# Four levels of a chunked recurrence: products over packed query columns

## What is computed

```python
b = jnp.cumsum(gc, axis=2)                       # log decays, summed inside a chunk
o = jnp.einsum('bhtk,bhkv->bhtv', qc * jnp.exp(b), s)
decay = jnp.exp(jnp.where(tri, b[:, :, :, None, :] - b[:, :, None, :, :], -jnp.inf))
att = jnp.einsum('bhtk,bhtsk,bhsk->bhts', qc, decay, kc)
o = o + jnp.einsum('bhts,bhsv->bhtv', att, vc)
s = jnp.exp(b_end)[..., None] * s + jnp.einsum('bhsk,bhsv->bhkv', kc * jnp.exp(b_end[:, :, None, :] - b), vc)
```

## Time and profile before

| | |
|---|---|
| median of 3 runs | 2225.09 us (2222.95 to 2227.34) |
| the profiled execution | 2226.52 us |
| its span | 2224.7 us |
| PE busy in the span | 2108.2 us (95%) |
| PEld, DVE, ACT, POOL busy | 85%, 51%, 36%, 40% |
| mean granted clock of PE | 0.974 |
| the recurrence (first product to last chunk of head 3) | 986.0 to 1096.9 us |

### The profile page before, as it was taken

The page is one execution under the profiler, slowest core; times in us unless marked ns, Lnnn a source line. Parts: engine busy times, 40 slices in busy tenths (PEclk is TensorE's granted clock), DMA queues, the critical chain, the costliest instruction groups (busy, mean ns, idle before and its releaser), DMA issues. The chain is left out here.

```text
span 2224.7 us, 38518 instructions
## 1 busy us (share of the span) xinstructions
PE 2108.2 (95%) x15606; PEld 1881.6 (85%) x15606; DVE 1145.7 (51%) x2132; ACT 793.7 (36%) x1654; POOL 880.8 (40%) x631
## 2 busy tenths in 40 slices
PE   5998999999999999998899999999999999999998
PEld 3997888856777689987899999678999999997886
DVE  5116545355676710258530054666865665654558
ACT  3203222234655611336412221234333333333553
POOL 2322121011111131211211223364388788776785
PEclk9999999988999999998899999999999999999999
DMA  7564534283100051100322130321244434357762
GB/s 267 193 214 160 183 121 152 92 304 139 32 32 11 1 143 39 39 9 3 99 76 57 47 125 4 117 95 41 86 162 151 139 132 166 129 182 284 266 226 105
DMA packets 152760, 268.23 MB, mean 121 GB/s; under 512 B 17817, under 2 KB 86348, under 8 KB 147975
## 3 DMA queue, kind: packets, MB, share of 16 engines
q1 hardware_dynamic: 144375, 222.70, 30.0%
q0 software_dynamic: 8208, 43.07, 5.5%
HBM read 211.93 MB, written 58.08 MB: 121 GB/s over the span
## 5 line engine op out<-in xcount | busy, mean ns | idle before, releaser
L3518 PE MATMUL PS<-down_parts 128*128 128x512 f32 x924 | 211.7, 390 | 1.1 <-DVE down_parts L4091 1.1
L3518 PEld LDWEIGHTS PS<-down_parts 128*128 128x128 f32 x924 | 173.1, 188 | 38.7 <-issue 2.0
L3475 PE MATMUL PS<-part_hi,w_ring 128*128 128x258 f32 x1152 | 192.3, 285 | 0.0
L3475 PEld LDWEIGHTS PS<-part_hi,w_ring 128*128 128x128 f32 x1152 | 162.1, 191 | 4.3 <-issue 4.3
L3475 PE MATMUL PS<-sum_blocks,w_ring 128*128 128x258 f32 x1296 | 161.6, 285 | 1.9 <-DVE out_sums L4041 1.9
L3475 PEld LDWEIGHTS PS<-sum_blocks,w_ring 128*128 128x128 f32 x1296 | 159.7, 192 | 2.1 <-DVE out_sums L4041 2.1
L651 POOL TENSOR_TENSOR w_merge_parts<-w_merge_raw,w_merge_parts 128x1024 fp32r<-128x1024 f32 x24 | 59.3, 2496 | 202.4 <-ACT w_merge_parts L644 183.6
L3867 POOL TENSOR_TENSOR down_parts<-down_raw,down_parts 128x512 fp32r<-128x512 f32 x71 | 118.5, 1686 | 43.2 <-ACT down_parts L3673 42.9
L2399 PE MATMUL PS<-h_hi,w_merge_parts 128*128 128x344 f32 x768 | 131.9, 324 | 0.0
L2399 PEld LDWEIGHTS PS<-h_hi,w_merge_parts 128*128 128x128 f32 x768 | 122.5, 189 | 3.1 <-issue 3.0
L1865 ACT ACTIVATE scores<-scores,mins_p 128x640 f32<-128x640 f32 (+5 forms) x192 | 112.5, 589 | 25.2 <-DVE mins_p L1907 24.4
(11 more groups left out here) (617 smaller groups left out, 5182.9 us busy)
## 6 DMA issues: line engine op xcount, KB each, us to landing
down_raw<-act_blocks SPq DMA_DIRECT2D x77, 256.0 KB, 3.4
w_or_ada<-w_ada SPq DMA_DIRECT2D x8, 2048.0 KB
w_raw<-w_up SPq DMA_DIRECT2D x11, 1024.0 KB, 9.4
w_raw<-w_gate SPq DMA_DIRECT2D x11, 1024.0 KB, 6.7
w_down_rows<-w_down SPq DMA_DIRECT2D x11, 1024.0 KB, 7.3
w_down_blocks<-w_down_sums SPq DMA_DIRECT2D x11, 1024.0 KB, 8.7
down_raw<-w_down_blocks SPq DMA_DIRECT2D x44, 256.0 KB, 4.0
act_blocks<-act_sums SPq DMA_DIRECT2D x10, 1024.0 KB, 5.1
```

What stands on the lines that cost most here:

```text
L3475: last = pe.matmul(out[:, c, :], r32(w[:, k, :]), r32(h[:, k, QUART * c:QUART * c + QUART]), start=first and k + i == 0, stop=k == 3 and i ...
L3518: last = pe.matmul(PS[:, t, c], r32(s[:, x, P * (t % 4):P * (t % 4) + P]), r32(s[:, y, c]), start=first and i == 0, stop=last_j and i == 2 ...
```

## The change

Levels 3 to 6 multiply each chunk's 128 columns of `X` by the query columns alone: the 64 columns that stand in the second halves of the blocks, read with strides (`pair_halves(...)[1]`). They are written side by side, 64 for each chunk, so a job's 8 outputs lie in one PSUM bank. Each of these levels' masks keeps only its query columns too (64 wide, behind the two masks of 128), and `pick` reads mask and PSUM packed, and writes into `att` with strides as before. Levels 0 to 2, 7 and 8, and the order of all work, stay.

```diff
-    lev = [lev[0] | lev[1] | lev[2]] + lev[3:] + [s == t]
-    c["c_levels"] = np.stack(lev, 1).astype(np.int32)
+    small = [x.reshape(P, -1, 2, h)[:, :, 1].reshape(P, P // 2) for x, h in zip(lev[3:], (8, 4, 2, 1))]
+    c["c_levels"] = np.concatenate([lev[0] | lev[1] | lev[2], s == t] + small, 1).astype(np.int32)
...
-        lev = at("levels", [P, LEV - 1, P], 139104, I32)
+        lev = at("levels", [P, 4 * P], 139104, I32)
...
+        HALFC = P // 2
...
-            sp.dma_start(lev[:, :, :], a["c_levels"][:, :, :]).then_inc(lev_in, 16)
+            sp.dma_start(lev[:, :], a["c_levels"][:, :]).then_inc(lev_in, 16)
...
                             out = PS[:, 2 * (U % 2) + c // 4, P * (c % 4):P * (c % 4) + P]
+                            if 3 <= w < 7:
+                                out = PS[:, 2 * (U % 2), HALFC * c:HALFC * c + HALFC].rearrange("p (n s) -> p n s", s=64 >> w)
...
                             elif w == 6:
-                                last = pe.matmul(out, kk[:, h, cc], X[:, n % 3, cc], start=True, stop=True)
+                                last = pe.matmul(out, kk[:, h, cc], pair_halves(X[:, n % 3, cc], w)[1], start=True, stop=True)
                             else:
-                                last = pe.matmul(out, X[:, n % 3, cc], X[:, n % 3, cc], start=True, stop=True)
+                                last = pe.matmul(out, X[:, n % 3, cc], pair_halves(X[:, n % 3, cc], w)[1], start=True, stop=True)
...
-                d, level = att[:, h % 2, :, :], lev[:, u, :].unsqueeze(1).to_broadcast([P, NT, P])
+                d = att[:, h % 2, :, :]
+                x = P if w == 7 else 0
+                level = lev[:, x:x + P].unsqueeze(1).to_broadcast([P, NT, P])
                 if w == 2:
                     d, level, src = (t[:, :, 16:] for t in (d, level, src))
                 elif w < 7:
-                    d, level, src = (t.rearrange("p c (n x s) -> p c n x s", x=2, s=64 >> w)[:, :, :, 1] for t in (d, level, src))
+                    d = d.rearrange("p c (n x s) -> p c n x s", x=2, s=64 >> w)[:, :, :, 1]
+                    level = lev[:, 2 * P + HALFC * (w - 3):2 * P + HALFC * (w - 2)].rearrange("p (n s) -> p n s", s=64 >> w).unsqueeze(1).to_broadcast([P, NT, HALFC // (64 >> w), 64 >> w])
+                    src = PS[:, 2 * (U % 2), :].rearrange("p (c n s) -> p c n s", c=NT, s=64 >> w)
```

## The result

The changed kernel takes 2252.73 us (median of 5 runs, 2246.38 to 2255.53) against 2225.09 us before: a ratio of 1.0123, with a 95% interval of 1.0102 to 1.0143. It is slower by 1.2%. The profiled execution took 2255.46 us, with a mean granted clock of 0.957 (0.974 before).

A forecast was written before the change was run, and what follows sets the result against it. Bound: two chains ending close together, PE to level 5 then ACT, and PE to level 7 then DVE. Terms -0.35 + 4.2 + 8.0 = +11.9 us gave 2238.4 us profiled, median 2237 us, range 2222 to 2248.

The forecast's parts named there:

- the number of lost heads: Later heads (1 to 3) staying at half clock from level 3 to level 7: 0 to 3, one taken as likeliest.
- -0.35: Levels 3 to 6 at full clock: weight loads set the pace, 0.07 us less per job, five jobs on the path.
- 4.2: Head 0: clock falls around levels 3 to 5, later levels run at half; 3.4 us for two levels, 5.1 for three.
- 8.0: Microseconds added by one later head that stays at half clock from level 3 to the end of level 7.
- two or three later heads: Rival: two or three of heads 1 to 3 stay at half clock; 2245 us or 2253 us, chance 0.20.
- a head that enters level 3 at half clock: Condition for a later head to stay slow: levels 3 to 6 have half the columns to climb back on.
- A head at full clock: Later heads entering the changed levels at full clock: 128-column chunks follow without a gap, so the clock was expected to hold.
- 22.4 us: Later head at half clock, level 3 to the end of level 7: this time in place of 14.0 us.
- the rows at 414 and 1147 us: Profile evidence elsewhere in the kernel: 64 columns and one column cost 107 ns alike, so weight loads set the pace.
- the rival by which the columns set the pace: Levels 3 to 6 take half of 1.78 us and the clock holds; 5.2 us faster, 2219.8 us, chance 0.07.
- The picks, masks and bank: Levels 3 to 6: shorter picks only lengthen DVE's waits, smaller masks and one PSUM bank change no wait; zero.
- The rule on idle gaps: Skill page blames gaps between matmul bursts; no new gap in PE, so unchanged clock; the prediction trusted the 414 us row instead.

The follow-up runs named there:

- the moved wait: The kernel before, with the wait for the stored state moved from a head's first state update to its second; 2225.41 us, 0.9999.
- with fillers: Changed kernel plus three unused 256-column products before levels 0, 1 of heads 1 to 3 and levels 3, 4 of head 0; 2228.51 us, 1.0024.
- with the clock held: Unused products before levels 0, 1 (heads 1 to 3) and 3, 4 (all heads), added to the changed kernel, 2222.01 us, and the kernel before, 2220.96 us.
- the first set of fillers: The kernel before plus three unused 256-column products ahead of levels 0 and 1 of heads 1 to 3; 2224.49 us, 0.9997.
- all of them: The kernel before plus unused 256-column products before levels 0, 1 of heads 1 to 3 and levels 3, 4 of all heads; 2220.96 us, 0.9974.

## Why the prediction was wrong

It said 2237 us, 2222 to 2248. The time is 2252.73, outside the range by 5 us: the direction and the mechanism were right, the number of lost heads was not.

- *The step that failed* is "So the number of such heads is 0 to 3, and I take one as the likeliest". It was three in the profiled execution. With three the same sum gives -0.35 + 4.2 + 3 x 8.0 = 27.85, 2254.4 us for the profiled execution, which took 2255.46. The rival "two or three later heads" with its 2253 us for three was thus the one that came true; I gave two or three heads a chance of 0.20 and left the case of three out of the range. That it meets the median to within 0.3 us is luck: the five runs lie between 2246.38 and 2255.53, the terms' errors cancel (head 0 cost 0.9 us more, the part behind head 3 took 0.7 us less), and only one run was profiled.
- *Why one was too few.* The prediction had the right condition, "a head that enters level 3 at half clock, as heads 2 and 3 do now", and the experiments bear it out. By this condition and its own rows two heads were to be lost, heads 2 and 3, and taking one was a discount without a row behind it. The third is head 1. Before, its clock fell at 1004.5, 3.2 us after the transposes of head 0, and was back before level 3, 10.9 us after them. After the change it fell at 1013.2, 4.3 us after the transposes, and level 3 began 11.3 us after them at half clock (1020.14, 3.65 us). In heads 2 and 3 the falls came 5.0 and 5.5 us after the transposes (1047.3 - 1042.33, 1081.5 - 1076.03), about as before (5.1 and 6.1), so nothing in a lost head helps the next one. That the delay of head 0 is what cost head 1 its early return is not shown, and one profile speaks against it: with heads 1 to 3 changed and head 0 not, the fall came earlier still, at 1000.50, and level 3 was entered at half clock all the same. With 128 columns throughout, head 1 entered level 3 at full clock in the profile before and at half in that of the moved wait (3.75 us), so its early return before was not a property of the kernel. What fixes when the clock falls and returns between levels 0 and 2 stays open.
- *A head at full clock.* "Each changed level is followed by a chunk of 128-column products and no gap, and I expect that to hold" is right for levels 5 and 6 (1.00 throughout) and held in head 2 of the kernel with heads 2 and 3 changed. It fails for levels 3 and 4, which have gaps at full clock (0.54 and 0.95 us in head 1 before), as the prediction itself says where they "wait for `X` from DVE": with fillers, head 1 fell there from full clock, while head 2 of the other kernel did not.
- *The price of a later head* was right: 8.0 taken; 8.1, 7.3 and 8.7 measured, 24.1 for three. From level 3 to the chunk behind level 7 I had 22.4 us; in head 1 it took 21.5 (1020.14 to 1041.66), as the clock came back inside level 7. *Head 0* was 4.2 taken, 5.1 measured (20.3 - 15.2): levels 5, 6 and 7 all ran at half clock, and most of level 4 too. That is the upper of the two values I had worked out (5.1).
- *The load pace.* Of the -0.35 nothing was seen: a job of 64 columns takes 1.73 to 1.82 us at full clock, one of 128 takes 1.78, and with the clock held the recurrence is 0.2 us shorter. The columns don't set it, as the rows at 414 and 1147 us said, and the rival by which the columns set the pace is out. At half clock I took 3.5 us; the start to start of two 64-column levels with a chunk between is 4.69 us in the trace after (1029.66 to 1034.35), which less 1.23 for the chunk is 3.46. Read to the start of its chunk, a level takes 3.31 us (1029.66 to 1032.97) and the chunk 1.38.
- *The picks, masks and bank* cost nothing, as said (masks only: 0.9999). The picks of levels 5 and 6 did not fall to 0.69 us, and with masks alone packed they take the same; what is left with strides is the write into `att`.
- *The rule on idle gaps.* The trace after has PE and PEld busy for 13.60 of 13.60 us at half clock. The Trainium skill, page TensorE: Matmul & The Clock Gate, section HAM oscillation — how this bites in real kernels, looks for the cause of a low clock in waits between bursts of matmuls, its example a wait for a DMA of about 3 to 5 us. The trace does not agree with that as the whole account: this stretch had no gap and stayed low, and in head 0 the clock held with waits of 1.37 and 1.44 us ahead of levels 3 and 4 of 128 columns and fell with 1.39 and 1.48 us ahead of those of 64. The prediction was right to let the row at 414 us weigh more. That the falls begin around waits is so here too, but they are shorter ones: 1.07 us before level 3 ahead of the fall in the kernel with fillers, 1.48 us before level 4 in head 0 after.

## What to carry to other kernels

Where weights change with every product, halving the moving columns leaves the time at full clock as it was and can cost the clock itself: look at the granted clock by stretches, and find the job in which it comes back after a gap, before making that job narrower. When a job is narrowed after the return and PE does not wait around it, nothing happened here; at full clock but with waits around it, the clock fell in head 0 each time and in one later head, while four others held. In the job of the return, each narrowed level runs on at half clock and all later waits shift with it. And if one unit of a repeated pattern can be lost, price the case in which all of them are, and keep it in the range.

## What was not expected of the hardware

- PE at half clock while never idle: 13.60 us of both matmul and weight load in 13.60 us (after), 25.9 and 25.1 of 27.2 us in head 1. Full weight loading neither kept the clock nor brought it back; in the later heads a level of 128 columns did, with the same loads.
- 128 columns and 64 columns with 128 x 128 float32 weights cost the same at full clock, 1.78 and 1.79 us for a job of 16.
- The predicated copy of 512 elements a partition took 0.68 to 0.72 us at levels 3 and 4 and 1.29 to 1.32 us at levels 5 and 6, with mask and source packed in all of them. Where the query columns stand in runs of 8 or 4 in the destination it is fast, in runs of 2 and 1 slow.
- Products on which nothing depends cost nothing in the kernel before: 0.9997 (0.9982 to 1.0011) with the first set of fillers, 0.9974 (0.9959 to 0.9989) with all of them. Both recurrences are 1.7 to 1.9 us shorter; the rest of the second one's gain is not explained.
- Taking 2.7 us out of the last part of the recurrence (18.2 to 15.5) moved neither the span (2223.8) nor the median by as much. In the profile the whole recurrence is 1.8 us shorter, as heads 1 to 3 took 0.8 us more together, and the rest of the kernel took 0.9 us more.
